# One tile of a 31-tap depthwise convolution: from GpSimd to TensorE, with diagonal stationary tiles

## The reference, cut to what matters

```
def hybrid_mix(h, ...):
    p = h @ w_in                                   # 21 tiles of 128 channels
    pa, pb, pc, pd = split(p)
    y_a = gate_b * causal_depthwise_conv(gate_c * xa, sc_conv_w)      # 3 taps, 256 channels
    y_b = spatial_gating(...)
    y_c = rwkv7_time_mix(pc, ...)                  # recurrence, done in chunks of 64 tokens
    z1, z2 = split(pd)
    zd = causal_depthwise_conv(z1 * sigmoid(z2), cm_conv_w) + cm_conv_b   # 31 taps, 256 channels
    y_d = silu(layer_norm(zd, cm_ln_w, cm_ln_b))
    return concat([y_a, y_b, y_c, y_d]) @ w_out
```

## Time and profile before

| | us |
|---|---|
| runs of the kernel before: median (lowest to highest of 3) | 2396.73 (2388.4 to 2397.73) |
| the profiled execution's own time | 2394.59 |
| its span | 2392.6 |
| granted clock over the span, as a share of 2.4 GHz | 0.944 |

### The profile page before, as it was taken

How to read it: one execution, slowest core, us unless ns; L and a number is a source line. 1 busy time by engine, 2 the same in 40 slices (tenths; PEclk the granted TensorE clock), 3 DMA queues, 4 the chain that set the end, 5 groups by cost and what they waited for, 6 DMA issues and landing times.

```text
span 2392.6 us, 26265 instructions
## 1 busy us (share of the span) xinstructions
PE 2251.3 (94%) x10308; PEld 1777.5 (74%) x10308; DVE 504.8 (21%) x1040; ACT 301.6 (13%) x679; POOL 139.1 (6%) x166
## 2 busy tenths in 40 slices
PE   8978899998878999999999979999999999789998
PEld 6755788887657888877777865777777778748776
DVE  0336200022642000220002453000100013731001
ACT  1114100010121000110002211000200012111001
POOL 0000000000000000000000190000000000820000
PEclk9966999999889999999999978999999999879999
DMA  6410244433212444334444302544554443014443
GB/s 251 145 35 1 99 156 149 150 131 114 71 36 87 151 150 155 130 134 151 152 155 136 112 1 88 174 151 152 197 170 150 155 137 131 10 58 163 149 155 118
DMA packets 81583, 299.46 MB, mean 125 GB/s; under 512 B 9120, under 2 KB 9248, under 8 KB 81248
## 3 DMA queue, kind: packets, MB, share of 16 engines
q1 hardware_dynamic: 80352, 293.87, 36.0%
q0 software_dynamic: 1152, 4.45, 0.5%
HBM read 296.98 MB, written 1.05 MB: 125 GB/s over the span
## 4 chain that ended last, share of the span: by engine, by line
PE 87%; DVE 4%; POOLq 3%; POOL 2%; ACT 2%; issue 1%; DVEq 0%; DMA 0%; ACTq 0%; SPq 0%
PE psum L282 45%; PE psum L467 12%; PE psum L264 10%; PE psum L1575 5%; PE psum L714 5%; PE psum L2062 3%; POOLq L1300 3%; PE psum L439 2%; PE psum L423 2%; POOL space L1301 2%; PE psum L1459 1%; PE psum L2380 1%; PE psum L348 1%; PE psum L1523 1%; DVE sq L576 0%
## 5 line engine op out<-in xcount | busy, mean ns | idle before, releaser
L282 PE MATMUL psum<-h,ring 128*128 128x256 f32 x2976 | 654.3, 379 | 0.0
L282 PEld LDWEIGHTS psum<-h,ring 128*128 128x128 f32 x2976 | 566.1, 190 | 105.7 <-issue 32.1
L282 PE MATMUL psum<-x,ring 128*128 128x256 f32 x1728 | 393.1, 385 | 17.9 <-ACT x L2411 7.1
L282 PEld LDWEIGHTS psum<-x,ring 128*128 128x128 f32 x1728 | 333.8, 193 | 67.1 <-issue 16.3
L264 PE MATMUL psum<-hid,ring 128*128 128x256 f32 x1024 | 231.1, 379 | 0.0
L264 PEld LDWEIGHTS psum<-hid,ring 128*128 128x128 f32 x1024 | 194.6, 190 | 26.5
L467 PE MATMUL psum<-ring,hid 128*128 128x512 f32 x448 | 201.4, 592 | 0.0
L467 PEld LDWEIGHTS psum<-ring,hid 128*128 128x128 f32 x448 | 85.1, 190 | 83.3 <-issue 80.4
L536 DVE TENSOR_TENSOR hid<-psum,hid_act 128x256 f32<-128x256 f32 x56 | 23.8, 425 | 568.8 <-ACT hid_act L521 568.8
L521 ACT ACTIVATE hid_act<-psum 128x256 f32<-128x256 f32 x88 | 33.7, 383 | 781.9 <-PE psum L282 729.0
L467 PE MATMUL psum<-ring,space 128*128 128x512 f32 x256 | 112.3, 592 | 0.0
(11 more groups left out here) (323 smaller groups left out, 1682.3 us busy)
## 6 DMA issues: line engine op xcount, KB each, us to landing
ring<-in_weights SPq DMA_DIRECT2D x552, 512.0 KB, 3.2
space<-in_gains POOLq DMA_DIRECT2D x6, 512.0 KB, 4.0
const<-in_consts SPq DMA_DIRECT2D x1, 1493.0 KB, 10.9
x<-in_x SPq DMA_DIRECT2D x1, 1024.0 KB, 4.9
out<-x SPq DMA_DIRECT2D x2, 512.0 KB, 2.6
space<-in_params POOLq DMA_DIRECT2D x2, 509.5 KB, 4.6
space<-in_params SPq DMA_DIRECT2D x1, 659.0 KB, 12.0
space<-in_positions SPq DMA_DIRECT2D x1, 128.0 KB, 13.4
```

Of the source, the lines that this page charges most:

```text
L282: last = pe.matmul(out, unit[:, i, :], rhs[:, i, :], start=(i == 0), stop=(i == KD - 1), skip_group_check=True)
```

## The change

GpSimd no longer does the 31 taps of tile 0. A tap becomes a product on TensorE: the stationary operand is a 128x128 matrix with the tap's 128 weights on its diagonal, the moving operand is `zs[:, 0, j:j + 256]`, and the 31 products add up in PSUM bank 3. ScalarE makes the diagonals by scaling the identity matrix with one weight for each partition, in a ring of four buffers (`DIAGS = 4`, in the buffer `m[9]`, which is idle then), with a semaphore each way. TensorE does 11 taps after tile 15 of the projection, 10 after tile 17 and 10 after tile 19. ScalarE copies the sum out with the bias, before it copies tile 20. The two waits for `zd` of GpSimd become waits for that copy (`conv_out`), and `before_ts`, the first to write bank 3 again, waits for it too. GpSimd still makes the input tile, the gain loads, the 3-tap convolution and `ya`, which it now reaches earlier.

```diff
+DIAGS = 4
-        self.pool = Steps(sem("mixer_convolutions"), "zd ya")
+        self.pool = Steps(sem("mixer_convolutions"), "zs0 ya")
+        self.diag = self.m[9][:, 0:DIAGS, :]
+        self.diag_ready, self.diag_used = sem("tap_diagonals_ready"), sem("tap_diagonals_used")
+        self.conv_out = sem("tap_sum_copied")
...
+        def convolve(third):
+            first, last = (0, 11, 21, CMW)[third:third + 2]
+            if third == 0:
+                pe.wait_ge(*at(s.act, "kk_std"))
+                pe.wait_ge(*at(s.pool, "zs0"))
+            for j in range(first, last):
+                pe.wait_ge(s.diag_ready, l * CMW + j + 1)
+                mm(k.bank(3)[:, 0, :], s.diag[:, j % DIAGS, :], s.zs[:, 0, j:j + T], j == 0, j == CMW - 1).then_inc(
+                    s.diag_used, 1)
...
+            if n in (15, 17, 19):
+                convolve((n - 15) // 2)
...
+        pe.wait_ge(s.conv_out, l + 1)
         two_groups("before_ts", [], 2, pair(s.at, s.bt))
...
             if c == 0:
-                pe.wait_ge(*at(s.pool, "zd"))
                 pe.wait_ge(*at(s.dve, "zd"))
                 channel_sums("zn", "sum", s.zd, "ones", 0)
...
+        def diagonals(first, last):
+            for j in range(first, last):
+                if j >= DIAGS:
+                    act.wait_ge(s.diag_used, l * CMW + j - DIAGS + 1)
+                act.activation(s.diag[:, j % DIAGS, :], k.c("ident"), ACT.Copy, scale=s.p("cm_conv_w", j)).then_inc(
+                    s.diag_ready, 1)
-        tiles_out(12, 16)
+        tiles_out(12, 14)
+        diagonals(0, DIAGS)
+        tiles_out(14, 16)
         act.wait_ge(*at(s.dve, "run"))
...
-        tiles_out(16, PROJ2)
+        diagonals(DIAGS, 11 + DIAGS)
+        tiles_out(16, 18)
+        diagonals(11 + DIAGS, 21 + DIAGS)
+        tiles_out(18, 20)
+        diagonals(21 + DIAGS, CMW)
+        act.wait_ge(s.diag_used, (l + 1) * CMW)
+        act.activation(s.zd[:, 0, :], k.bank(3)[:, 0, :], ACT.Identity, bias=s.p("cm_conv_b", 0)).then_inc(s.conv_out, 1)
+        tiles_out(20, PROJ2)
...
             if c == 0:
+                dve.wait_ge(s.conv_out, l + 1)
                 centre("zn", s.zd, 0, T)
...
-        pool.tensor_tensor(s.zs[:, 0, CMW - 1:], s.z[:, 0, :], s.sz[:, 0, :], ALU.mult)
+        pool.tensor_tensor(s.zs[:, 0, CMW - 1:], s.z[:, 0, :], s.sz[:, 0, :], ALU.mult).then_inc(*s.pool.mark("zs0"))
         pool.drain()
         pool.wait_ge(*at(s.dve, "before.0"))
         load_gain(3 * l + 1)
-        conv(s.zs, "cm_conv_w", CMW, s.zd, 1)
-        pool.drain()
-        pool.tensor_scalar(s.zd[:, 0, :], s.zd[:, 0, :], s.p("cm_conv_b", 0), None, ALU.add).then_inc(
-            *s.pool.mark("zd"))
```

## The result

| | before | after |
|---|---|---|
| median of the runs (lowest to highest), us | 2394.86 (2388.4 to 2397.73), 4 runs | 2415.3 (2412.93 to 2418.08), 4 runs |
| profiled execution's own time, us | 2394.59 | 2414.47 |

The changed kernel is slower: ratio 1.0079, interval 1.0058 to 1.0101, which is 14 to 24 us. Forecast was 2414 us, 19.5 us more than the profiled execution before; the two profiled executions differ by 19.9 us.

A forecast was written before the change was run, and what follows sets the result against it. TensorE was taken to bound the projection, with VectorE ending its long gaps in the chunk matrices. The terms 26.8 - 2.9 - 4.4 = 19.5 us on 2394.59 gave 2414.1 us; forecast's range 2409 to 2420, 8 in 10 range 2404 to 2426.

The forecast's parts named there:

- Added products: Projection, bound by TensorE: 62 tap products of 0.432 us add their full time, 26.8 us over two layers.
- Diagonals hide: Projection: ScalarE makes the diagonals beside TensorE's taps at zero cost, with 0 to 2.6 us as the bound.
- the bound of 1.3 us a layer: Projection: worst cost if nothing overlaps, 19 diagonals a layer each taking 0.50 us against a product's 0.432.
- The loop: Projection: one round of a diagonal buffer through ScalarE and TensorE, put at 1.32 us against 1.73 for four products.
- The increments' rule: Tap products: serialized completion increments of about 26.3 ns each would add 1.6 us, giving 2415.6; left out of the sum.
- Removed wait, 2.9 us: Before `zn.sum`: TensorE's whole wait for GpSimd goes, 0.87 us in layer 1 and 2.06 in layer 2.
- relieved VectorE, 4.4 us: Chunk matrices and recurrence: VectorE work ahead of TensorE's gaps quickens without GpSimd's taps, 2.0 us in layer 1, 2.4 in layer 2.
- so nothing changes there: Right after the projection: GpSimd's 3-tap work slows VectorE's first masks and taps just as the 31 taps did.
- The bound of 8.8 us for VectorE alone: Upper bound of VectorE's relief, if all 30 taps of a layer and two other operations lay on the path.
- The clock at nothing, with 3.2 us either way: Work after the projection, shifted by 13.4 us: one clock fall more or less is about 1.6 us; zero taken.
- a return of the clock: From the gap before `na` through recurrence and output products: 2.4 GHz kept, up to 36 us saved, 2378 us; chance 0.06.
- The sign on the clock: Sign to look for in the changed profile: the granted clock after `x3` is still 0.50.

The follow-up runs named there:

- products_alone: Kernel before, GpSimd's taps kept, plus 31 unused products with the identity in each layer's projection, without diagonals or increments: 2426.93 us, ratio 1.0117.
- ring2: Changed kernel with two diagonal buffers in place of four: 2421.97 us, ratio 1.0124 to the kernel before.
- ring8: Changed kernel with eight diagonal buffers in place of four: 2418.27 us, ratio 1.0084 to the kernel before.
- after_fill: Changed kernel plus 24 unused products in TensorE's gaps of each layer's chunk matrices: 2403.85 us, ratio 1.0024 to the kernel before.
- before_fill: Kernel before, GpSimd's taps kept, plus 4, 13 and 7 unused products in TensorE's gaps of the chunk matrices: 2396.08 us, ratio 0.9997.
- pool_early: Kernel before with GpSimd's 31 taps begun earlier, in the middle of the projection, and the gain row loaded after them: 2387.55 us, ratio 0.9952.
- both_early: Kernel before with GpSimd's taps begun early and VectorE's tile 1 taps moved into and just behind the projection: 2372.26 us, ratio 0.9883.

## Why the prediction was right

- *Added products.* 62 x 0.432 = 26.8 us: measured 13.4 us a layer in the projection, twice. The step held, with `products_alone` as its own test.
- *Diagonals hide.* Held: no gap at a tap. Of the bound of 1.3 us a layer nothing came. The loop is 1.19 us, not 1.32. Tile 20 follows tile 16 by three tiles and two thirds of the taps, 19 us, and not by two tiles and one third as I wrote; the copy had more room still.
- *The increments' rule.* The estimate of 1.6 us more, from the Trainium skill ("TensorE: Matmul & The Clock Gate", "The cost: per-tile semaphore tail"), did not come: the thirds with and without increments are equal to 0.01 us. The page states its 26.3 ns for small tiles packed side by side in the array; here full products follow one another 0.432 us apart.
- *Removed wait, 2.9 us, and relieved VectorE, 4.4 us, together 7.3.* TensorE's gaps shrank by 7.0 (7.1 and 6.9 in `ring2` and `ring8`). The wait gave its 2.9. The gap behind n3 shrank by 1.11 in layer 1 (0.93 forecast) and the wait for L1262 in the recurrence from 1.82 to 1.11 (0.70 forecast); with layer 2 and the gap behind x3, 4.7 us. Against that, the gap ahead of the group p4 grew from 1.89 to 2.30 and from 1.81 to 2.08 us, 0.7 together. I had put this at nothing ("so nothing changes there"), but beside the 3-tap work VectorE's two masks of line 1205 (1238 in the changed kernel) take 1.83 us in layer 1, where beside the 31 taps they took 1.43. The bound of 8.8 us for VectorE alone, towards which the lock of the Trainium skill ("SBUF — State Buffer", "SBUF: two separate sides") pointed, did not come: the median tap was held up by 57 ns, not by a whole GpSimd operation.
- *The clock at nothing, with 3.2 us either way.* It gave 2.0 us in the profiled executions. `na` took 1.25 and 1.15 us for 1.99 and 2.03, so the clock fell later behind x3 in both layers, as it did in `ring2` and `ring8` (1.14 and 1.15). But the sum of such falls is scatter: TensorE's busy time in the mixing stages, 206.3 us before and 204.3 in the changed kernel, is 204.7 in `ring2` and 207.1 in `ring8`, with the same program there; a gain of 2.0 to a loss of 0.8. This term is where 19.5 in the sum and 17.8 in the stages (26.8 - 9.0) part. I had called a return of the clock a rival of 0.06 that would need 2.4 GHz through the whole recurrence; `after_fill` shows that the part up to the start of the recurrence is worth some 4 us a layer and can be had.
- *Luck in the total.* The stages make 17.8 us; the 19.9 of the profiled executions, so near to 19.5, holds 2.1 us from the identical part ahead. By the medians the change costs 20.4 us. The range was kept by the terms, the last half microsecond by chance.
- *The sign on the clock.* The granted clock behind x3 was forecast to stay at 0.50; from `na` to the products of `out` it is 0.51 and 0.52.
- *What I had not seen.* I read the small wait for GpSimd as its price. It was the height of a floor, and `before_fill` shows that the floor swallowed the gain ahead of it, all of it. For this change the sum is the same, since it removed the floor and relieved VectorE at once.

## What to carry to other kernels

Work moved to the busiest engine costs its full time in a stage that this engine bounds, and little or nothing in its gaps elsewhere; so choose the place by the gaps before choosing the engine. The wait that an idle-looking engine causes tells how far its path sticks out now, and the next gain ahead of it may go into that wait. Before moving work off a slow engine, see whether it can merely begin earlier: here that shortened the mixing stages by 8.0 us, where the change shortened them by 9.0, and cost nothing in the projection.

## What the runs showed of the hardware

Products in a gap made a stage shorter although they added 10 us of TensorE time to it: at a granted clock of 0.52, about 1.2 GHz, `na` takes 1.99 us (kernel before), at 1.00, 2.4 GHz, it takes 1.15 (`after_fill`).

The granted clock also goes with most of the difference between executions of identical work. Of the 70 executions of the kernel before that were run beside the experiments, the 12 with a mean granted clock from 0.948 to 0.950 took 2387.4 to 2388.4 us, and the 23 with 0.940 to 0.942 took 2399.1 to 2402.8 us. Part of this is there before the first mixer that was changed: TensorE reaches the transpose ahead of it at 1276.72 us before, at 1269.40 in `pool_early` and at 1283.68 in `both_early`, whose programs are the same up to there. In the stretch from 600 to 900 us of those two the granted clock was 0.96 and 0.92, though the slower one is then also at an earlier point of the program. An effect of 5 us is below this spread in single executions, and was readable only stage by stage.
